# Hybrid attention block on one core: ring slots of 4352 bytes, a running sum of squares, and reordered score products

## The chip, the core and the metric

The kernel runs on one core of a Trainium2 chip. The core has a matrix engine (TensorE, PE in the rows; its weight loads are PEld), a vector engine (VectorE, DVE), an activation engine (ScalarE, ACT), GpSimd (POOL) and SyncE (SP), which here only issues the large loads. The engines run side by side, each through its own list of instructions, and wait for each other by semaphores. The metric is the time of one execution on the device in microseconds (us), lower is better.

## The reference, cut to what matters

```python
D_MODEL, SEQ, DEPTH = 2048, 256, 1            # one layer, one sequence of 256 tokens, fp32
h = rmsnorm(x, g_norm)                        # needs the sum of the squares of x, per token
z = einsum('bsd,dn->bsn', h, w_in)            # 2048 -> 12296 columns
# 8 heads of differential attention: q and k are two maps of 64 dims, v has 128
s = einsum('bqhmd,bkhmd->bhmqk', q, k) * scale ; p = softmax(causal(s))
a = p[:, :, 0] - lam * p[:, :, 1] ; oa = rmsnorm(a @ v, g_subln) * (1 - lam_init) * silu(ga)
# 8 heads of forgetting attention: q, k, v have 128 dims, a bias of cumulative log-forget gates
ob = softmax(causal(q @ k.T * scale + c_q - c_k)) @ v * silu(gb)
m = sigmoid(ma) * (oa @ w_proj_a) + sigmoid(mb) * (ob @ w_proj_b)
return rmsnorm(x + m @ w_out, g_final)
```

Queries are taken in two blocks of 128. The first block sees 128 keys, the second 256, so a map of scores is one block of 128x128 and one of 128x256.

## The kernel before, in words

**Precision.** Nearly all products are made three times with a rounded type (fp32r): both operands are split into a high part and a low part, and high x high, high x low and low x high are added in PSUM. That is `split_product` (lines 216 to 219): three matmuls, L217, L218 and L219. A few small products (transposes, values, sums) are plain fp32, for which the trace shows two weight loads and two matmul records each.

**The weight ring.** Weights come as tiles, numbered t = 0 to 255. A tile is 4096 bytes in each of 128 partitions (two blocks of 128 rows x 512 columns), and feeds 12 matmuls of 512 columns: 2 blocks, 2 halves of the tokens, 3 products. Tiles 8 to 11 hold 4 x 264 columns (4224 bytes), tiles 12 to 15 hold 4 x 256, each with 24 matmuls. Three buffers, `w_raw`, `w_hi` and `w_lo`, have four slots each, and tile t uses slot t % 4. SP loads tile t once VectorE has finished tile t-4 (`load`, line 186), ScalarE rounds it to `w_hi` once TensorE has finished tile t-4 (`split`, L421), VectorE subtracts to `w_lo` (`split`, L610), then TensorE uses both. A slot is `SLOT` elements long, the length of the longest tile: 1056, or 4224 bytes. In the built program `w_raw` begins 128 bytes past a multiple of 256, and so do `w_hi`, `w_lo`, `hT_hi` and `hT_lo` (the stationary operands) and `oT_hi` and `oT_lo`. 4224 is an odd multiple of 128. So slots 0 and 2 begin 128 past a multiple of 256, and slots 1 and 3 at a multiple of 256. Tiles 248 to 251, the first half of the last column block, are copied from the ring into `oT_hi` and `oT_lo` (L569, L817) and read there; their length in that buffer is 4096 bytes, so all four begin 128 past a multiple of 256.

**The first column block** (tiles 0 to 7, matmuls at L340) runs while x arrives. For each pair of row blocks ScalarE makes `hT_hi` (`x_part`, L433) and the tile's `w_hi`, VectorE makes `hT_lo` (L623) and `w_lo`. After that ScalarE squares all of x into `x_sq`, 8 pieces of 512 columns (L445; `x_sq` lies in the buffer `gates`), among the splits of tiles 8 to 11. VectorE adds the 16 blocks with one reduction (L641) to `x_ssq`. TensorE, between tiles 8 and 9, multiplies `x_ssq` by ones to sum over the partitions (L351). From this come `ms` (VectorE, L644) and `rstd` (GpSimd, L866), which every eviction of the first block needs.

**The column blocks c = 2 to 23** (8 tiles each) are the heads' projections and the merge gates. `attention(c, j)` puts the work of older heads between the tiles: after tile j = 1 the transposes, after tile j = 5 the products with the values of head c-3 (`values`, L285, 6 records) and the scores of head c-2 (`scores`, line 255). Heads 0 to 7 are the forgetting heads: one map, into PSUM bank B. Heads 8 to 15 are the differential heads: two maps, q and k in partitions 0 to 63 and 64 to 127, into banks B and C, the whole of B first. `head_qkT` (ScalarE, L474) and `head_qkT_lo` (VectorE, L693) make the high and low part of q and k of a head from bank A, 512 columns: q of both blocks, k of both blocks.

After that come 4 column blocks of the branch projections and 4 of the output projection, the last of them in another order (line 397).

Of the kernel before, what the change touches and what calls it, by code (L numbers as in the profile page):

```python
# [8 lines left out]
P = 128  # L9
D_MODEL = 2048  # L10
SEQ = 256
M_TILES = SEQ // P
KT = D_MODEL // P
HEADS = 8
HD = 128
QK = 64
# [5 lines left out]
CHUNK = 512  # L22
RING = 4
TILES = 8
Z_SLOTS = 3
FL_COLS = 2 * HD + HEADS
SLOT = 4 * FL_COLS
FL_COL = 8 * WIDTH
MERGE_COL = FL_COL + HEADS
N_HEADS = 2 * HEADS  # L30
# [11 lines left out]
def build(nc, x, xT, g_cols, consts_in, w_main, w_fl, g_final, out):  # L42
    fp32 = mybir.dt.float32
    fp32r = mybir.dt.float32r
    ALU = mybir.AluOpType
    ACT = mybir.ActivationFunctionType
    AX = mybir.AxisListType
# [6 lines left out]
    with ctx:  # L54
        def sb(name, shape, dt=fp32):
            return ctx.enter_context(nc.sbuf_tensor(name, shape, dt))
# [23 lines left out]
        lam_exp = sb("lam_exp", [P, 2])  # L80
        neg_half = sb("neg_half", [P, M_TILES])
        neg_lam = sb("neg_lam", [P, 1])
        x_ssq = sb("x_ssq", [P, SEQ])
        ms = sb("ms", [P, M_TILES])
        rstd = sb("rstd", [P, M_TILES])
        half_rstd = sb("half_rstd", [P, M_TILES])
# [2 lines left out]
        log_f = sb("log_f", [P, M_TILES, HEADS])  # L89
        c_nat = sb("c_nat", [P, M_TILES, HEADS])  # L90
        c_neg = sb("c_neg", [HEADS, SEQ])
        qkT_hi = sb("qkT_hi", [P, 4 * P], fp32r)
        qkT_lo = sb("qkT_lo", [P, 4 * P], fp32r)
        bias = sb("bias", [P, 3 * P])
        rope_t = sb("rope_t", [P, 4, M_TILES, 4, ROPE_HALF])
        probs = sb("probs", [P, 2, 3 * P])
# [21 lines left out]
        ones = consts[:, C_ONE:C_ONE + P]  # L118
# [6 lines left out]
        xT_sb = x_sb[:].rearrange("p (k n) -> p k n", k=KT)  # L125
        x_res = x_sb[:].rearrange("p (m n) -> p m n", m=M_TILES)
        x_sq = gates[:, 0, :].rearrange("p (k n) -> p k n", k=KT)
# [10 lines left out]
        A, B, C, Dk = bank("A"), bank("B"), bank("C"), bank("Dk")  # L138
# [12 lines left out]
        xh_ready, xl_ready, x_squared, x_summed = sem("xh_ready"), sem("xl_ready"), sem("x_squared"), sem("x_summed")  # L151
# [9 lines left out]
        qkT_done, qkT_hi_ready, qkT_ready = sem("qkT_done"), sem("qkT_hi_ready"), sem("qkT_ready")  # L161
# [9 lines left out]
        out_ready, out_stored = [sem("out_ready0"), sem("out_ready1")], sem("out_stored")  # L171

        def width(t):
            return SLOT if 8 <= t < 12 else 2 * CHUNK

        def raw_count(t):
            return 16 * (t // RING + 1)
# [37 lines left out]
        def _(pe):  # L215
            def split_product(acc, a_hi, a_lo, b_hi, b_lo, first, last):
                pe.matmul(acc, a_hi, b_hi, start=first, stop=False)  # L217
                pe.matmul(acc, a_hi, b_lo, start=False, stop=False)  # L218
                return pe.matmul(acc, a_lo, b_hi, start=False, stop=last)  # L219
# [35 lines left out]
            def scores(h):  # L255

                pe.wait_ge(qkT_ready, h + 1)
                if h >= 2:
                    pe.wait_ge(oT_lo_ready, h - 1)
                maps = 1 if h < HEADS else 2  # L260
                for i in range(maps):
                    part = slice(0, P) if maps == 1 else slice(i * QK, (i + 1) * QK)
                    S = (B, C)[i]
                    split_product(S[:, 0:P], qkT_hi[part, 0:P], qkT_lo[part, 0:P],
                                  qkT_hi[part, 2 * P:3 * P], qkT_lo[part, 2 * P:3 * P], True, True)
                    mm = split_product(S[:, P:3 * P], qkT_hi[part, P:2 * P], qkT_lo[part, P:2 * P],
                                       qkT_hi[part, 2 * P:4 * P], qkT_lo[part, 2 * P:4 * P], True, True)
                mm.then_inc(scores_done, 1)

            def prob_transposes(h):  # L270
# [54 lines left out]
            for j in range(TILES):  # L325
                hi, lo = k_view(w_hi, j, 2, CHUNK), k_view(w_lo, j, 2, CHUNK)
                for part, (x_part, w_part) in enumerate(((hT_hi, hi), (hT_lo, hi), (hT_hi, lo))):
                    for kk in range(2):
# [10 lines left out]
                        for m in range(M_TILES):  # L339
                            mm = pe.matmul(Z[m][:], x_part[:, 2 * j + kk, m * P:(m + 1) * P], w_part[:, kk],  # L340
                                           start=(j == 0 and part == 0 and kk == 0),
                                           stop=(j == TILES - 1 and part == 2 and kk == 1))
                mm.then_inc(w_used, 1)
            for j in range(4):
                tile(8 + j, 1, hT_hi, hT_lo, 4 * j, 4, FL_COLS, j == 0, j == 3)
                if j == 0:

                    pe.wait_ge(x_summed, 1)
                    pe.wait_ge(consts_loaded, 16)
                    for m in range(M_TILES):  # L350
                        mm = pe.matmul(A[:, m:m + 1], x_ssq[:, m * P:(m + 1) * P], ones[:, 0:1], start=True, stop=True)  # L351
                    mm.then_inc(ms_done, 1)
            banks_free(2)
            for j in range(4):
# [1 line left out]
            for c in range(2, PROJ):  # L356
                banks_free(fill_of(c))
                for j in range(TILES):
# [7 lines left out]
                    if c == 2 and j == 1:  # L366
                        pe.wait_ge(c_nat_ready, 1)
                        for m in range(M_TILES):
                            mm = pe.matmul(C[0:HEADS, m * P:(m + 1) * P], c_nat[:, m, :], ident, start=True, stop=True)
# [27 lines left out]
            for part, (m, y_cols, acc) in enumerate(LAST):  # L397
                tok = slice(m * P, (m + 1) * P)
                n = y_cols.stop - y_cols.start
                cols = slice(y_cols.start - 3 * CHUNK, y_cols.stop - 3 * CHUNK)  # L400
                for j in range(TILES):
                    t = 8 * (OUT + 3) + j
# [4 lines left out]
                    for kk in range(2):  # L407
                        k = 2 * j + kk
                        mm = split_product(acc[:, 0:n], hT_hi[:, k, tok], hT_lo[:, k, tok], hi[:, kk, cols],
                                           lo[:, kk, cols], k == 0, k == KT - 1)  # L410
# [3 lines left out]
        def _(act):  # L414
            def split(t):

                if t >= RING:
                    act.wait_ge(w_used, t - RING + 1)
                act.wait_ge(raw_loaded[t % RING], raw_count(t))
                n = width(t)  # L420
                act.activation(w_hi[:, t % RING, 0:n], w_raw[:, t % RING, 0:n], ACT.Copy).then_inc(hi_ready, 1)  # L421
# [6 lines left out]
            def x_part(j):  # L428

                act.wait_ge(x_loaded[j], 16)  # L430
                for kk in range(2):
                    k = 2 * j + kk
                    act.activation(hT_hi[:, k, :], xT_sb[:, k, :], ACT.Copy, scale=g_col[:, k:k + 1]).then_inc(xh_ready, 1)  # L433

            act.dma_start(g_col[:], g_cols).then_inc(g_loaded, 16)
            act.wait_ge(warm_ready, 1)
            act.activation(table_probe[:], warm[:, 0:1], ACT.Copy)
# [3 lines left out]
            for j in range(1, TILES):  # L441
                x_part(j)
                split(j)
            for j in range(TILES):
                act.activation(x_sq[:, 2 * j:2 * j + 2, :], xT_sb[:, 2 * j:2 * j + 2, :], ACT.Square,  # L445
                               scale=D_MODEL ** -0.5).then_inc(x_squared, 1)
                if j < 4:
                    split(8 + j)

            act.wait_ge(rstd_ready, 1)  # L450
            evacuate(0)
# [19 lines left out]
            def head_qkT(h):  # L471

                act.wait_ge(qkT_done, h + 1)
                act.activation(qkT_hi[:], A[:], ACT.Copy).then_inc(qkT_hi_ready, 1)  # L474

            def head_pT(h):
                act.wait_ge(pT_done, h + 1)
# [83 lines left out]
            for n in range(3):  # L561
                for j in range(TILES):
                    if n == 0 and j == 2:
                        merged_hi(3)
                    t = 8 * (OUT + n) + j + RING
# [26 lines left out]
        def _(dve):  # L592
# [13 lines left out]
            def split(t):  # L606

                dve.wait_ge(hi_ready, t + 1)
                n = width(t)
                dve.tensor_tensor(w_lo[:, t % RING, 0:n], w_raw[:, t % RING, 0:n], w_hi[:, t % RING, 0:n].bitcast(fp32),  # L610
                                  ALU.subtract).then_inc(lo_ready, 1)
# [6 lines left out]
            def x_part(j):  # L618

                for kk in range(2):  # L620
# [2 lines left out]
                    dve.scalar_tensor_tensor(hT_lo[:, k, :], xT_sb[:, k, :], g_col[:, k:k + 1], hT_hi[:, k, :].bitcast(fp32),  # L623
                                             ALU.mult, ALU.subtract).then_inc(xl_ready, 1)

            dve.memset(warm[:], 0.0).then_inc(warm_ready, 1)
            dve.memset(o_scale[:, 0:1], 0.5)
            dve.wait_ge(g_loaded, 16)
            for j in range(TILES):
# [5 lines left out]
                    dve.tensor_copy(w_hi[:, 0, CHUNK:2 * CHUNK], w_raw[:, 0, CHUNK:2 * CHUNK]).then_inc(hi_ready, 1)  # L635
                x_part(j)
                split(j)
            for j in range(3):
                split(8 + j)
            dve.wait_ge(x_squared, 8)  # L640
            dve.tensor_reduce(x_ssq[:], x_sq.rearrange("p k n -> p n k"), AX.X, ALU.add).then_inc(x_summed, 1)  # L641
            split(11)
            dve.wait_ge(ms_done, 1)
            dve.tensor_scalar(ms[:], A[:, 0:M_TILES], EPS, None, ALU.add).then_inc(ms_ready, 1)  # L644
            dve.wait_ge(rstd_ready, 1)
# [44 lines left out]

            def head_qkT_lo(h):
                dve.wait_ge(qkT_hi_ready, h + 1)
                dve.tensor_tensor(qkT_lo[:], A[:], qkT_hi[:].bitcast(fp32), ALU.subtract).then_inc(qkT_ready, 1)  # L693

            def gate_product(h):

# [286 lines left out]
```

## Time and profile before

| | us |
|---|---|
| median of 3 runs | 785.65 |
| lowest, highest | 785.4, 786.19 |
| the profiled execution, its own time | 785.83 |
| its span, first to last instruction | 784.0 |

| engine | busy us | share of the span |
|---|---|---|
| TensorE matmul | 766.0 | 98% |
| TensorE weight load | 633.1 | 81% |
| VectorE | 428.8 | 55% |
| ScalarE | 364.5 | 46% |
| GpSimd | 67.8 | 9% |

The profile gives busy time and the chain of work that ended last, of which TensorE has 95%. The mean clock granted to TensorE is 0.99 of full speed. Matmul records overlap (a record of 0.39 us begins 0.23 us after the one before), so what a matmul costs is read from start to start in the order of time, never from its duration.

### The profile page before, as it was taken

How to read it: one execution, taken by the hardware profiler on the slowest of the kernel's cores; microseconds unless marked ns; L12 is line 12 of the kernel's file. 1: busy time of each engine (PE TensorE's matmuls, PEld its weight loads, DVE VectorE, ACT ScalarE, POOL GpSimd, SP SyncE). 2: the span in 40 equal slices, each digit the busy share in tenths (PEclk: the TensorE clock that was granted, in tenths of full speed). 3: DMA queues.
4: the chain of work that ended last, by engine and by line, in shares of the span. 5: the costliest groups of instructions: out<-in, count | busy, mean ns of one | idle time of the engine just before them, and what ended most of it. 6: DMA issues, size and time to landing. Idle time of an engine off the chain costs nothing.

```text
span 784.0 us, 9598 instructions
## 1 busy us (share of the span) xinstructions
PE 766.0 (98%) x3652; PEld 633.1 (81%) x3652; DVE 428.8 (55%) x610; ACT 364.5 (46%) x540; POOL 67.8 (9%) x153
## 2 busy tenths in 40 slices
PE   8699999999999999999999999999999999999996
PEld 5598888888888888888888888888888888888886
DVE  6645555555555565666656564444444665655562
ACT  6535444444444454455455554434444434444441
POOL 0000200000001110222022000000000000001110
PEclk9989999999999999999999999999999999999998
DMA  8626655555555545645445545555555555865542
GB/s 320 217 82 218 238 169 179 168 174 171 170 178 169 175 164 165 183 159 168 162 161 183 163 164 187 187 190 188 188 188 188 191 186 187 308 210 186 189 154 108
DMA packets 39885, 143.80 MB, mean 183 GB/s; under 512 B 4568, under 2 KB 4576, under 8 KB 39328
## 3 DMA queue, kind: packets, MB, share of 16 engines
q1 hardware_dynamic: 39152, 140.85, 53.7%
q0 software_dynamic: 256, 1.54, 0.5%
q10 hardware_dynamic: 432, 0.79, 0.3%
q8 instruction: 30, 0.49, 0.3%
q14 instruction: 15, 0.12, 0.0%
HBM read 141.06 MB, written 2.11 MB: 183 GB/s over the span
## 4 chain that ended last, share of the span: by engine, by line
PE 95%; issue 2%; DVE 1%; DMA 1%; ACT 1%; SPq 0%; DVEq 0%; POOLq 0%; POOL 0%; ACTq 0%
PE Z L217 29%; PE Z L219 29%; PE Z L218 29%; PE Z L340 3%; PE A L285 1%; PE A L251 1%; DVE x_ssq L641 1%; DMA w_raw<-in_w_main 1%; PE Dk L276 1%; PE B L217 1%; PE B L218 0%; PE C L294 0%; PE B L219 0%; ACT gates L445 0%; ACT w_hi L421 0%
## 5 line engine op out<-in xcount | busy, mean ns | idle before, releaser
L610 DVE TENSOR_TENSOR w_lo<-w_raw,w_hi 128x1024 fp32r<-128x1024 f32 (+1 forms) x252 | 311.4, 1237 | 315.0 <-ACT w_hi L421 313.2
L421 ACT ACTIVATE w_hi<-w_raw 128x1024 fp32r<-128x1024 f32 (+1 forms) x247 | 261.9, 1061 | 364.9 <-PE Z L219 354.8
L217 PE MATMUL Z<-w_hi,hT_hi 128*128 128x512 f32 (+2 forms) x880 | 341.5, 388 | 0.5 <-DVE w_lo L610 0.5
L219 PE MATMUL Z<-w_hi,hT_lo 128*128 128x512 f32 (+2 forms) x880 | 338.7, 385 | 0.0
L218 PE MATMUL Z<-w_lo,hT_hi 128*128 128x512 f32 (+2 forms) x880 | 338.1, 384 | 0.0
L219 PEld LDWEIGHTS Z<-w_hi,hT_lo 128*128 128x128 f32 x880 | 166.2, 189 | 34.8
L217 PEld LDWEIGHTS Z<-w_hi,hT_hi 128*128 128x128 f32 x880 | 166.5, 189 | 34.3 <-issue 0.6
L218 PEld LDWEIGHTS Z<-w_lo,hT_hi 128*128 128x128 f32 x880 | 166.4, 189 | 33.4
L217 PE MATMUL Z<-w_hi,oT_hi 128*128 128x512 f32 x128 | 50.5, 394 | 0.0
L219 PE MATMUL Z<-w_hi,oT_lo 128*128 128x512 f32 x128 | 50.3, 393 | 0.0
L218 PE MATMUL Z<-w_lo,oT_hi 128*128 128x512 f32 x128 | 50.2, 392 | 0.0
L900 POOL TENSOR_TENSOR rope_t<-z_sb,consts 128x32 f32<-128x32 f32 x64 | 26.9, 453 | 88.1 <-DVE z_sb L615 48.4
L923 POOL TENSOR_TENSOR gates<-gates,rows 128x512 f32<-128x512 f32 x6 | 7.7, 1302 | 267.8 <-DVE gates L808 267.8
L219 PEld LDWEIGHTS Z<-w_hi,oT_lo 128*128 128x128 f32 x128 | 24.0, 188 | 5.5
L218 PEld LDWEIGHTS Z<-w_lo,oT_hi 128*128 128x128 f32 x128 | 24.0, 188 | 5.4
L217 PEld LDWEIGHTS Z<-w_hi,oT_hi 128*128 128x128 f32 x128 | 24.1, 188 | 5.3
L881 POOL TENSOR_TENSOR bias<-rows,c_nat 128x128 f32<-128x128 f32 (+1 forms) x16 | 7.7, 504 | 139.7 <-DVE neg_max L686 134.4
L916 POOL TENSOR_TENSOR o_rstd<-o_ms,neg_half 128x2 f32<-128x2 f32 x8 | 5.6, 702 | 119.2 <-DVE o_ms L764 119.2
L553 ACT ACTIVATE z_sb<-gates 128x512 f32<-128x512 f32 (+1 forms) x9 | 5.2, 579 | 22.7 <-DVE gates L834 13.9
L285 PEld LDWEIGHTS A<-z_sb,pT 128*128 128x128 f32 x96 | 13.1, 190 | 1.5
L425 ACT ACTIVATE z_sb<-Z,rstd 128x512 f32<-128x512 f32 x15 | 10.0, 668 | 9.2 <-POOL rstd L866 9.2
L285 PE MATMUL A<-z_sb,pT 128*128 128x128 f32 x96 | 13.3, 274 | 0.0
(155 smaller groups left out, 493.5 us busy)
## 6 DMA issues: line engine op xcount, KB each, us to landing
w_raw<-in_w_main SPq DMA_DIRECT2D x251, 512.0 KB, 3.3
w_raw<-in_w_fl SPq DMA_DIRECT2D x4, 528.0 KB, 5.2
x_sb<-in_xT SPq DMA_DIRECT2D x8, 256.0 KB, 6.4
x_sb<-in_x SPq DMA_DIRECT2D x1, 2048.0 KB, 11.2
rows<-c_rows_dram POOLq DMA_DIRECT2D x1, 1024.0 KB, 5.8
rows<-in_g_final SPq DMA_DIRECT2D x1, 1024.0 KB, 12.6
out_y<-gates SPq DMA_DIRECT2D x2, 384.0 KB, 2.5
out_y<-gates ACTq DMA_DIRECT2D x2, 384.0 KB, 3.5
```

What stands on the lines that cost most here:

```text
L217: pe.matmul(acc, a_hi, b_hi, start=first, stop=False)
L218: pe.matmul(acc, a_hi, b_lo, start=False, stop=False)
L219: return pe.matmul(acc, a_lo, b_hi, start=False, stop=last)
L251: mm = pe.transpose(A[:, (2 * i + m) * P:(2 * i + m + 1) * P], z_sb[:, h % Z_SLOTS, m, i * HD:(i + 1) * HD], ident)
L276: mm = pe.transpose(Dk[:, b * P:(b + 1) * P], probs[:, 0, b * P:(b + 1) * P], ident)
L285: mm = pe.matmul(A[:, q * P:(q + 1) * P], pT[:, b * P:(b + 1) * P], z_sb[:, h % Z_SLOTS, k, 2 * HD:3 * HD], start=b < 2, stop=b != 1)
L340: mm = pe.matmul(Z[m][:], x_part[:, 2 * j + kk, m * P:(m + 1) * P], w_part[:, kk], start=(j == 0 and part == 0 and kk == 0), stop=(j == TI ...
L421: act.activation(w_hi[:, t % RING, 0:n], w_raw[:, t % RING, 0:n], ACT.Copy).then_inc(hi_ready, 1)
L425: act.activation(z_sb[:, c % Z_SLOTS, 0], Z[2 * (fill_of(c) % 2)][:], ACT.Copy, scale=rstd[:, 0:1]).then_inc(evac[0], 1)
L610: dve.tensor_tensor(w_lo[:, t % RING, 0:n], w_raw[:, t % RING, 0:n], w_hi[:, t % RING, 0:n].bitcast(fp32), ALU.subtract).then_inc(lo_ready, 1)
L641: dve.tensor_reduce(x_ssq[:], x_sq.rearrange("p k n -> p n k"), AX.X, ALU.add).then_inc(x_summed, 1)
L900: ins = pool.tensor_tensor(rope_t[:, i, m], u, v, ALU.mult)
```

## The change

`SLOT` goes from 1056 to 1088 elements, from 4224 to 4352 bytes, 17 x 256; the tiles' lengths stay. All slots now begin 128 bytes past a multiple of 256. `x_ssq` has two blocks of 256 columns. ScalarE squares two row blocks at a time inside the first column block (`x_square`), VectorE adds each piece to `x_ssq` (`x_sum`, 7 adds of 512 columns) in place of the reduction, and TensorE's product with ones follows tile 9 in place of tile 8, with two matmuls for each half of the tokens in place of one. In `scores`, the block of 128x128 is one plain fp32 matmul of `qk0T`, a new copy of q and k of the first block, in place of three fp32r matmuls; the 128x256 block keeps its three, and for differential heads the matmuls of B and C alternate. `head_qkT` writes `qk0T` (256 columns) and a `qkT_hi` of 384 columns, `head_qkT_lo` a `qkT_lo` of 384.

```diff
-SLOT = 4 * FL_COLS
+SLOT = 1088
...
-                maps = 1 if h < HEADS else 2
-                for i in range(maps):
-                    part = slice(0, P) if maps == 1 else slice(i * QK, (i + 1) * QK)
-                    S = (B, C)[i]
-                    split_product(S[:, 0:P], qkT_hi[part, 0:P], qkT_lo[part, 0:P],
-                                  qkT_hi[part, 2 * P:3 * P], qkT_lo[part, 2 * P:3 * P], True, True)
-                    mm = split_product(S[:, P:3 * P], qkT_hi[part, P:2 * P], qkT_lo[part, P:2 * P],
-                                       qkT_hi[part, 2 * P:4 * P], qkT_lo[part, 2 * P:4 * P], True, True)
+                parts = [slice(0, P)] if h < HEADS else [slice(0, QK), slice(QK, 2 * QK)]
+                for S, part in zip((B, C), parts):
+                    pe.matmul(S[:, 0:P], qk0T[part, 0, :], qk0T[part, 1, :], start=True, stop=True)
+                for n, (q, k) in enumerate(((qkT_hi, qkT_hi), (qkT_hi, qkT_lo), (qkT_lo, qkT_hi))):
+                    for S, part in zip((B, C), parts):
+                        mm = pe.matmul(S[:, P:3 * P], q[part, 0:P], k[part, P:3 * P], start=n == 0, stop=n == 2)
...
-                if j == 0:
-
-                    pe.wait_ge(x_summed, 1)
+                if j == 1:
+
+                    pe.wait_ge(x_summed, TILES - 1)
                     pe.wait_ge(consts_loaded, 16)
                     for m in range(M_TILES):
-                        mm = pe.matmul(A[:, m:m + 1], x_ssq[:, m * P:(m + 1) * P], ones[:, 0:1], start=True, stop=True)
+                        for i in range(2):
+                            mm = pe.matmul(A[:, m:m + 1], x_ssq[:, i, m * P:(m + 1) * P], ones[:, 0:1], start=i == 0, stop=i == 1)
...
-                act.activation(qkT_hi[:], A[:], ACT.Copy).then_inc(qkT_hi_ready, 1)
+                act.activation(qk0T[:], A[:].rearrange("p (i n) -> p i n", i=2)[:, :, 0:P], ACT.Copy)
+                act.activation(qkT_hi[:], A[:, P:4 * P], ACT.Copy).then_inc(qkT_hi_ready, 1)
...
+            def x_sum(j):
+
+                dve.wait_ge(x_squared, j + 1)
+                if j > 1:
+                    dve.wait_ge(x_summed, j - 1)
+                before = x_sq[:, 0:2, :] if j == 1 else x_ssq[:]
+                dve.tensor_tensor(x_ssq[:], before, x_sq[:, 2 * j:2 * j + 2, :], ALU.add).then_inc(x_summed, 1)
...
-            for j in range(3):
+                if j > 3:
+                    x_sum(j - 3)
+            for j in range(4):
                 split(8 + j)
-            dve.wait_ge(x_squared, 8)
-            dve.tensor_reduce(x_ssq[:], x_sq.rearrange("p k n -> p n k"), AX.X, ALU.add).then_inc(x_summed, 1)
-            split(11)
+                if j < 3:
+                    x_sum(j + 5)
```

On VectorE, from the last split of the first column block on, the program stood like this (128x1056 are the splits of tiles 8 to 11):

```order
20 L610 TENSOR_TENSOR w_lo<-w_raw,w_hi 128x1024
21 L610 TENSOR_TENSOR w_lo<-w_raw,w_hi 128x1056 x3
22 L641 TENSOR_REDUCE x_ssq<-gates 128x256
23 L610 TENSOR_TENSOR w_lo<-w_raw,w_hi 128x1056
24 L644 TENSOR_SCALAR ms<-A 128x2
```

and now, from the fifth tile (t = 4) on:

```order
14 L617 TENSOR_TENSOR w_lo<-w_raw,w_hi 128x1024
15 L639 TENSOR_TENSOR x_ssq<-gates 128x512
16 L630 SCALAR_TENSOR_TENSOR hT_lo<-x_sb,g_col,hT_hi 128x256 x2
17 L617 TENSOR_TENSOR w_lo<-w_raw,w_hi 128x1024
18 L639 TENSOR_TENSOR x_ssq<-x_ssq,gates 128x512
...
29 L617 TENSOR_TENSOR w_lo<-w_raw,w_hi 128x1056
30 L639 TENSOR_TENSOR x_ssq<-x_ssq,gates 128x512
31 L617 TENSOR_TENSOR w_lo<-w_raw,w_hi 128x1056
32 L660 TENSOR_SCALAR ms<-A 128x2
```

The one reduction ahead of the split of tile 11 has become seven adds, one behind each split of tiles 4 to 10.

On TensorE, the scores of a differential head, before:

```order
1142 L285 MATMUL A<-z_sb,pT 128x128 x3
1143 L217 MATMUL B<-qkT_hi 128x128
1144 L218 MATMUL B<-qkT_lo,qkT_hi 128x128
1145 L219 MATMUL B<-qkT_hi,qkT_lo 128x128
1146 L217 MATMUL B<-qkT_hi 128x256
1147 L218 MATMUL B<-qkT_lo,qkT_hi 128x256
1148 L219 MATMUL B<-qkT_hi,qkT_lo 128x256
1149 L217 MATMUL C<-qkT_hi 128x128
1150 L218 MATMUL C<-qkT_lo,qkT_hi 128x128
1151 L219 MATMUL C<-qkT_hi,qkT_lo 128x128
1152 L217 MATMUL C<-qkT_hi 128x256
1153 L218 MATMUL C<-qkT_lo,qkT_hi 128x256
1154 L219 MATMUL C<-qkT_hi,qkT_lo 128x256
```

and now:

```order
1126 L284 MATMUL A<-z_sb,pT 128x128 x3
1127 L263 MATMUL B<-qk0T 128x128
1128 L263 MATMUL C<-qk0T 128x128
1129 L266 MATMUL B<-qkT_hi 128x256
1130 L266 MATMUL C<-qkT_hi 128x256
1131 L266 MATMUL B<-qkT_lo,qkT_hi 128x256
1132 L266 MATMUL C<-qkT_lo,qkT_hi 128x256
1133 L266 MATMUL B<-qkT_hi,qkT_lo 128x256
1134 L266 MATMUL C<-qkT_hi,qkT_lo 128x256
1135 L218 MATMUL Z<-w_hi,hT_hi 128x512
```

Twelve matmuls of one bank after the other have become two plain fp32 matmuls (two records each in a trace) and six fp32r matmuls that alternate between the banks.

## Rows read from the trace of the kernel before

**Rows 1.** Page, part 1: busy time, share of the span, instructions of each engine.

```profile
PE 766.0 (98%) x3652; PEld 633.1 (81%) x3652; DVE 428.8 (55%) x610; ACT 364.5 (46%) x540; POOL 67.8 (9%) x153
```

**Rows 2.** Waits of TensorE, longest first: total us, times, longest us.

```profile
PE A L351 <- DVE x_ssq L641: 7.4, 1, 7.4
```

**Rows 3.** Order of time, 20 to 42 us: start, duration, engine, line, idle before.

```profile
20.08 1.21 DVE L610 TENSOR_TENSOR w_lo<-w_raw,w_hi 128x1024 fp32r<-128x1024 f32 x1
...
22.01 1.21 DVE L610 TENSOR_TENSOR w_lo<-w_raw,w_hi 128x1024 fp32r<-128x1024 f32 x1
...
31.14 2.17 ACT L445 ACTIVATE gates<-x_sb 128x512 f32<-128x512 f32 x4
...
33.35 7.00 DVE L641 TENSOR_REDUCE x_ssq<-gates 128x256 f32<-128x4096 f32 x1 [3.61 <-ACT gates L445]
...
40.41 1.02 PE L351 MATMUL A<-consts,x_ssq 128*128 128x1 f32 x4 [7.39 <-DVE x_ssq L641]
41.29 0.57 PE L217 MATMUL Z<-w_hi,hT_hi 128*128 128x264 f32 x1
```

**Rows 4.** Order of time, TensorE: first matmuls of tiles 10, 11 and 12.

```profile
46.46 0.28 PE L217 MATMUL Z<-w_hi,hT_hi 128*128 128x264 f32 x1
...
49.40 0.28 PE L217 MATMUL Z<-w_hi,hT_hi 128*128 128x264 f32 x1
...
52.35 0.28 PE L217 MATMUL Z<-w_hi,hT_hi 128*128 128x256 f32 x1
```

**Rows 5.** Stretches: us, busy of PE, PEld, DVE, ACT, POOL, PEclk, DMA share, GB/s.

```profile
41.00:44.00 3.00, 3.00 (x14) 3.00 (x15) 1.44 (x4) 1.47 (x2) 0.72 (x1) 0.50 0.48 152
48.00:52.00 4.00, 4.00 (x35) 4.00 (x34) 0.00 (x0) 0.00 (x0) 0.00 (x0) 1.00 0.02 5
```

**Rows 6.** Order of time, TensorE: first matmuls of tiles 240, 241 and 242.

```profile
732.07 0.39 PE L217 MATMUL Z<-w_hi,hT_hi 128*128 128x512 f32 x1
...
734.80 0.40 PE L217 MATMUL Z<-w_hi,hT_hi 128*128 128x512 f32 x1
...
737.60 0.39 PE L217 MATMUL Z<-w_hi,hT_hi 128*128 128x512 f32 x1
```

**Rows 7.** Same view, the last column block: starts of tiles 249, 250, 253, 254.

```profile
755.55 0.39 PE L217 MATMUL Z<-oT_hi,hT_hi 128*128 128x512 f32 x1
...
756.91 0.39 PE L217 MATMUL Z<-oT_hi,hT_hi 128*128 128x512 f32 x1
...
760.99 0.40 PE L217 MATMUL Z<-w_hi,hT_hi 128*128 128x512 f32 x1
...
762.38 0.39 PE L217 MATMUL Z<-w_hi,hT_hi 128*128 128x512 f32 x1
```

**Rows 8.** Same view, values and scores of forgetting heads.

```profile
130.98 0.83 PE L285 MATMUL A<-z_sb,pT 128*128 128x128 f32 x6
131.56 0.31 PE L217 MATMUL B<-qkT_hi 128*128 128x128 f32 x1
...
132.34 0.40 PE L217 MATMUL Z<-w_hi,hT_hi 128*128 128x512 f32 x1
```

**Rows 9.** Same view, values and scores of differential heads.

```profile
403.80 0.83 PE L285 MATMUL A<-z_sb,pT 128*128 128x128 f32 x6
404.56 0.32 PE L217 MATMUL B<-qkT_hi 64*128 64x128 f32 x1
...
404.84 0.32 PE L217 MATMUL C<-qkT_hi 64*128 64x128 f32 x1
404.94 0.33 PE L217 MATMUL B<-qkT_hi 64*128 64x256 f32 x1
...
405.52 0.28 PE L219 MATMUL C<-qkT_hi,qkT_lo 64*128 64x256 f32 x1
405.72 0.50 PE L217 MATMUL Z<-w_hi,hT_hi 128*128 128x512 f32 x1
```

**Rows 10.** Groups by line and shape: busy us, mean ns of one, idle before.

```profile
L693 DVE TENSOR_TENSOR qkT_lo<-A,qkT_hi 128x512 fp32r<-128x512 f32 x16 | 10.8, 676 | 0.0
...
L478 ACT ACTIVATE pT<-Dk 128x384 f32<-128x384 f32 x16 | 7.7, 482 | 0.0
```

More of the change, by code:

```diff
@@ L82, in build @@
         neg_lam = sb("neg_lam", [P, 1])
-        x_ssq = sb("x_ssq", [P, SEQ])
+        x_ssq = sb("x_ssq", [P, 2, SEQ])
         ms = sb("ms", [P, M_TILES])
@@ L91, in build @@
         c_neg = sb("c_neg", [HEADS, SEQ])
-        qkT_hi = sb("qkT_hi", [P, 4 * P], fp32r)
-        qkT_lo = sb("qkT_lo", [P, 4 * P], fp32r)
+        qk0T = sb("qk0T", [P, 2, P])
+        qkT_hi = sb("qkT_hi", [P, 3 * P], fp32r)
+        qkT_lo = sb("qkT_lo", [P, 3 * P], fp32r)
         bias = sb("bias", [P, 3 * P])
@@ L173, in width @@
         def width(t):
-            return SLOT if 8 <= t < 12 else 2 * CHUNK
+            return 4 * FL_COLS if 8 <= t < 12 else 2 * CHUNK
         def raw_count(t):
@@ L433, in x_part, with x_square @@
                     act.activation(hT_hi[:, k, :], xT_sb[:, k, :], ACT.Copy, scale=g_col[:, k:k + 1]).then_inc(xh_ready, 1)
+            def x_square(j):
+                act.activation(x_sq[:, 2 * j:2 * j + 2, :], xT_sb[:, 2 * j:2 * j + 2, :], ACT.Square,
+                               scale=D_MODEL ** -0.5).then_inc(x_squared, 1)
             act.dma_start(g_col[:], g_cols).then_inc(g_loaded, 16)
@@ L443, in _ @@
                 split(j)
[L444 to L448, printed above, removed]
+                if j > 1:
+                    x_square(j - 2)
+            for j in range(4):
+                if j < 2:
+                    x_square(j + TILES - 2)
+                split(8 + j)
             act.wait_ge(rstd_ready, 1)
@@ L624, in x_part @@
                                              ALU.mult, ALU.subtract).then_inc(xl_ready, 1)
+            def x_sum(j):
+                dve.wait_ge(x_squared, j + 1)
+                if j > 1:
+                    dve.wait_ge(x_summed, j - 1)
+                before = x_sq[:, 0:2, :] if j == 1 else x_ssq[:]
+                dve.tensor_tensor(x_ssq[:], before, x_sq[:, 2 * j:2 * j + 2, :], ALU.add).then_inc(x_summed, 1)
             dve.memset(warm[:], 0.0).then_inc(warm_ready, 1)
@@ L637, in _ @@
                 split(j)
-            for j in range(3):
+                if j > 3:
+                    x_sum(j - 3)
+            for j in range(4):
                 split(8 + j)
-            dve.wait_ge(x_squared, 8)
-            dve.tensor_reduce(x_ssq[:], x_sq.rearrange("p k n -> p n k"), AX.X, ALU.add).then_inc(x_summed, 1)
-            split(11)
+                if j < 3:
+                    x_sum(j + 5)
             dve.wait_ge(ms_done, 1)
@@ L692, in head_qkT_lo @@
                 dve.wait_ge(qkT_hi_ready, h + 1)
-                dve.tensor_tensor(qkT_lo[:], A[:], qkT_hi[:].bitcast(fp32), ALU.subtract).then_inc(qkT_ready, 1)
+                dve.tensor_tensor(qkT_lo[:], A[:, P:4 * P], qkT_hi[:].bitcast(fp32), ALU.subtract).then_inc(qkT_ready, 1)
             def gate_product(h):
```

## The prediction

> **What bounds the kernel now.** First the page: TensorE is busy for 766.0 of 784.0 us, the next engine for 55% of them [rows 1]. So a change pays where it shortens TensorE's own row of work, or an idle stretch in it. The waits come next: TensorE has one long one, 7.4 us, for the sum of squares [rows 2]. The order of time tells why. ScalarE ends its last squares at 33.3, VectorE's reduction starts at 33.35 and takes 7.00, and TensorE begins the product with ones at 40.41 [rows 3]. Then I look at what TensorE is granted: behind that idle stretch the clock is 0.50, which is 1.2 GHz, and from 48 us on it is 1.00, which is 2.4 GHz [rows 5]. The same 24 matmuls that take 2.94 and 2.95 us in tiles 10 and 11 (46.46 to 49.40 to 52.35) take 5.17 in tile 9 (41.29 to 46.46) [rows 3, 4]. Last come the steady tiles, from first matmul to first matmul. Tile 240 (slot 0) takes 2.73 us, tile 241 (slot 1) 2.80 with the same 12 matmuls [rows 6]; unrounded, the starts of the 20 tiles from 228 on give 2.735 and 2.792 in turn, with no wait between. This is the largest thing that the busy shares hide.
>
> **1. Slots of 4352 bytes.** Is it the slot's address that costs the odd tiles 0.057 us, or their place in the operands, which alternates in the same way? The last column block answers. Tile 249 is odd, but is read from another buffer, 128 bytes past a multiple of 256 like slots 0 and 2; six of its matmuls take 1.36 us (755.55 to 756.91). Tile 253, also odd, is read from slot 1, and six take 1.39 (760.99 to 762.38) [rows 7]. The address it is, and the two fast kinds (slots 0 and 2) lie 256 apart modulo 512, so that a multiple of 256 between slots is enough. The bases of the three ring buffers and of the stationary operands keep their place modulo 256. All four slots then are of the fast kind. Odd tiles of 512 columns in the ring: 124 from t = 1 to 247, less 9, 11, 13 and 15 with narrower matmuls (even and odd alike there [rows 4]) = 120. 120 x 0.057 = 6.8, and 0.06 in tiles 253 and 255: **-6.9 us**. All of it is on the path, since the rows of TensorE have no gaps there. Bounds: 0, if it isn't the address after all, and -6.9. I take -6.9, by [rows 7].
> By the Trainium skill ("TensorE: Matmul & The Clock Gate", section "Back-to-back issue gap") a matmul of N columns follows the one before by N/2.4 + 2.5 ns at full clock, 216 ns at 512, with no word on addresses. Here it is 228 in one kind of slot and 233 in the other, so no run here agrees with it; by that rule the slots would bring nothing.
>
> **2. The sum of squares.** Removed: the stretch without work, 7.5 us (tile 8 would be over at about 32.9, the product starts at 40.41), and the slow tile 9, 5.17 - 2.94 = 2.2 us. Added on TensorE: the product with ones is 4 records, 0.88 us from 40.41 to 41.29 at the low clock [rows 3], and is now 8 records. At full clock a plain fp32 record of 128 weights takes 0.112 (six in L285 and six in the scores fill 1.36 us [rows 8]), so 8 x 0.112 = 0.9, as much as before; the other bound is 8 x 0.22 = 1.8, if the low clock came back.
> Is something late in place of the reduction? *ScalarE* has one piece of squares more in each step, 2.17 / 4 = 0.54 [rows 3]. Its step and VectorE's are both 1.93 us (20.08 to 22.01), so its becomes 2.47. *VectorE* gets an add of 512 columns. The trace has none from SBUF alone; the nearest row is a subtraction of 512 with one operand in PSUM, 0.68 [rows 10], the upper bound the one of 1024, 1.21 [rows 3]. I take 0.6 from start to start: 2.53. TensorE needs 2.74 a tile, so both still keep ahead. In full: VectorE ended tile 7's split at 23.2 and will at about 25.9 (ScalarE's five squares more are 2.7 us); TensorE wants that tile's low part at 28.9. ScalarE waits for TensorE to release the slots of tiles 10 and 11 anyway, so these splits stay at about 28.5 to 29.9 and 30 to 31. The seventh add ends at about 32.3, and TensorE is through tile 9 at 35.6: 3.3 us to spare. With adds at 1.2 each the sum would be 4.2 us later, 0.9 too late. The loads of tiles 8 to 11, queued on SP behind VectorE's splits, go out 1.1 to 2.7 us later; what uses them has 3 us. Behind tile 9 `ms`, `rstd` and the two evictions take some 2.5 us and run under tiles 10 and 11 (5.9 us), with room for the split of tile 12. From tile 12 on the order is the old one, shifted. TensorE gets there at 42.4 in place of 52.35; 0.2 of that belongs to part 1. **-9.7 us**, bounds -10 and -8.
>
> **3. The fp32 block, forgetting heads.** From the first record of the values to the tile behind the scores it is 1.36 us [rows 8] for 12 records, 0.113 each, 128 or 256 columns alike. One fp32 matmul is two records, three fp32r are three: one record less, 8 x -0.113 = **-0.9 us**. Two copies on ScalarE (256 columns at about 0.46, 384 at 0.48 [rows 10]) take the place of one, 0.3 us more for each head, but the scores come four tiles later, and VectorE's subtraction gets shorter. Cost nothing.
>
> **4. Differential heads.** The values start at 403.80 and the next tile at 405.72: 1.92 us for 6 + 12 records [rows 9]. C's first matmul starts at 404.84, ahead of B's fourth (404.94), though it stands behind it in the program. So two halves of the array do run side by side, but C lags B by 0.28. Now each bank has 5 records. Around them stands what I keep [rows 9]: values' last record at 404.35; 0.20 to 0.25 to the first score; 0.20 from the last score's start (405.52) to the tile. If C follows B by one record (0.112), it is 0.25 + 4 x 0.112 + 0.112 + 0.20 = 1.02 in place of 1.37 (404.35 to 405.72): -0.35 for a head. With no lag -0.46 to -0.51, with the old lag of 0.28 -0.18, with no overlap at all (10 records in a row, 1.47) +0.1. I take one record, since B's two fp32 records stand ahead of C's in the program: 8 x -0.35 = **-2.8 us**, bounds -4.1 and +0.8.
> The Trainium skill says (same page, "Part 3: Packing small matmuls", "The mechanism") that matmuls start strictly in program order, and those on different row groups some 4 ns apart. The order of time contradicts the first half [rows 9]. By the second the pairs would start together, and this part would be at its bound, 1.3 us below my sum.
>
> **Sum.** -6.9 - 9.7 - 0.9 - 2.8 = -20.3. The profiled execution took 785.83 in all, 784.0 of it span; 785.83 - 20.3 = 765.5. The median of the runs lies 0.2 lower: **765.4 us**.
>
> **Rivals.**
> *A. The alternating scores don't overlap.* In its favour: entering the half-array products and leaving them costs 0.1 us more than a record each time [rows 9], and alternation could pay something like it often. Against: B and C overlap already. Part 4 is +0.8: 769.0. Chance 0.13.
> *B. The slots bring nothing*, because it is another relation between ring and stationary operand that counts. For: four slots become four addresses modulo 1024, of which the trace shows two. Against: the pair of odd tiles [rows 7]. 765.4 + 6.9 = 772.3. Chance 0.07. With it goes the case that the change doesn't do what it says and makes all slots slow, 779: 0.02.
> *C. Slower than before: TensorE starves in the first column block and loses its clock.* If VectorE's add took over 0.81 us, its step would exceed 2.74 and every tile from 4 on would wait. A wait alone is cheap, under 2 us in all. But at 1.2 GHz, half the clock, a tile of 512 columns takes up to twice its 2.74 us: six tiles at +2.5 and four narrow ones at +2.2 (part 2) are 24 us, and 765.4 + 24 = 789. It decides at that 0.81, and only if short waits lower the clock. Against: 0.68 is the dearer kind [rows 10], and only a wait of 7.4 us has brought the low clock. Chance 0.02.
>
> **Numbers.** My forecast has the chance 0.76, from 763.6 (no lag, and a little more) to 768 (old lag, late adds, dear product). With A the range of 763.6 to 770.0 leaves out B, C and a tail, some 15%. A measurement of this kernel can tell about 0.2% from no change, 1.6 us; every case but C is below that. Faster 0.97, same 0.01, slower 0.02.
>
> **What would show it.** In the changed kernel's order of time: tiles of odd number at 2.735 us like even ones (part 1; 2.79 or other values in some slots would be B). No wait of TensorE for `x_ssq`, a clock of 1.00 from 33 to 52 us and tile 12 at about 42.4 (part 2; a wait between tiles 4 and 9 would be the start of C). 1.24 us from the values to the tile for a forgetting head (part 3), about 1.57 for a differential one, with C's first record about 0.11 behind B's (part 4; 2.0 would be A). I would be wrong if a wait that the 7.4 us has covered so far came up, such as that for the constants' load, or if the ring's loads, closer together now, landed late.

## The result and the profile after

| | before | after |
|---|---|---|
| median of 4 runs each, us | 785.66 | 762.18 |
| lowest, highest | 785.4, 786.19 | 761.63, 764.31 |
| profiled execution: own time, span | 785.83, 784.0 | 761.63, 759.8 |

The ratio is 0.9705, with a 95% interval of 0.9686 to 0.9725: 23.5 us less. The forecast was 765.4 with a range of 763.6 to 770.0. The sign and the four sources were right, but the time lies 1.4 us below the range, so the forecast was wrong in size. Of the runs reported below, one of the slots alone (1549 us) and one of the kernel before beside it (4355 us) fell far out of line, and medians, ratios and intervals are of the others.

The page of the changed kernel begins like this (busy time of each engine, then the longest wait of TensorE; its line numbers differ by a few from those before, L218 to L220 are the three products):

```profile
PE 749.2 (99%) x3632; PEld 627.0 (83%) x3632; DVE 422.8 (56%) x616; ACT 365.9 (48%) x556; POOL 76.2 (10%) x153
```

```profile
PE Dk L322 <- DVE warm L641: 1.3, 1, 1.3
```

The wait of 7.4 us [rows 2] is gone and none has taken its place: the longest is 1.3 us, at the very start, and behind the first column block there is one of 0.44 us, ahead of tile 13. In the order of time, the product with ones and the first matmuls of tiles 10, 11 and 12 (start, duration):

```profile
34.83 0.95 PE L351 MATMUL A<-consts,x_ssq 128*128 128x1 f32 x8
35.63 0.37 PE L218 MATMUL Z<-w_hi,hT_hi 128*128 128x264 f32 x1
...
38.66 0.28 PE L218 MATMUL Z<-w_hi,hT_hi 128*128 128x264 f32 x1
...
41.56 0.29 PE L218 MATMUL Z<-w_hi,hT_hi 128*128 128x256 f32 x1
```

Tile 12 starts at 41.56, where it started at 52.35 [rows 4]. In the view of stretches (us, busy of PE, PEld, DVE, ACT, POOL, granted clock, DMA share, GB/s) the clock of this part is full, 2.4 GHz, where it was 0.50 [rows 5]:

```profile
33.00:36.00 3.00, 3.00 (x28) 3.00 (x27) 0.16 (x1) 0.00 (x0) 0.00 (x0) 1.00 0.70 251
41.00:44.00 3.00, 3.00 (x27) 3.00 (x27) 1.08 (x4) 1.74 (x4) 0.00 (x0) 1.00 0.44 160
```

The first matmuls of tiles 240, 241 and 242, which answer to [rows 6]:

```profile
708.26 0.39 PE L218 MATMUL Z<-w_hi,hT_hi 128*128 128x512 f32 x1
...
710.98 0.39 PE L218 MATMUL Z<-w_hi,hT_hi 128*128 128x512 f32 x1
...
713.70 0.39 PE L218 MATMUL Z<-w_hi,hT_hi 128*128 128x512 f32 x1
```

Both tiles take 2.72 us. The odd one has lost 0.07, and the even one 0.015, which I had not forecast. With the stage boundaries of both traces the difference can be laid out, in us:

| from, to | before | after | difference | in my sum |
|---|---|---|---|---|
| start, tile 1 | 10.50 | 9.87 | -0.63 | 0 |
| tile 1, tile 12 | 41.85 | 31.69 | -10.16 | -9.9 |
| tile 12, tile 248 | 701.82 | 688.47 | -13.36 | -10.3 |
| tile 248, end of the span | 29.84 | 29.80 | -0.04 | -0.1 |

The difference of the two spans is 24.2 us, 0.7 more than that of the medians. Of the 3.9 us by which my sum of 20.3 falls short of 24.2, 3.1 are in the steady tiles, 0.6 ahead of tile 1 and 0.3 between tiles 1 and 12.

### The profile page after: what moved, and what is told of

The parts are those of the page before. It is cut to its first block, busy times and chain, and to the rows that moved or that the text cites. A ratio compares the mean times of both kernels' runs of the same rounds, so it can differ in the third digit from the quotient of the medians.

```text
span 759.8 us, 9586 instructions
## 1 busy us (share of the span) xinstructions
PE 749.2 (99%) x3632; PEld 627.0 (83%) x3632; DVE 422.8 (56%) x616; ACT 365.9 (48%) x556; POOL 76.2 (10%) x153
## 4 chain that ended last, share of the span: by engine, by line
PE 96%; issue 2%; DMA 1%; DVE 0%; ACT 0%; SPq 0%; DVEq 0%; POOLq 0%; POOL 0%; ACTq 0%
PE Z L218 29%; PE Z L220 29%; PE Z L219 29%; PE Z L339 3%; PE A L284 1%; PE A L252 1%; DMA w_raw<-in_w_main 1%; PE B L266 1%; PE Dk L275 1%; PE B L263 1%; PE C L293 0%; ACT w_hi L421 0%; PE A L301 0%; PE B L301 0%; DVE w_lo L617 0%
## 5 line engine op out<-in xcount | busy, mean ns | idle before, releaser
L218 PE MATMUL Z<-w_hi,hT_hi 128*128 128x512 f32 (+2 forms) x880 | 337.8, 384 | 0.4 <-DVE w_lo L617 0.4
L220 PE MATMUL Z<-w_hi,hT_lo 128*128 128x512 f32 (+2 forms) x880 | 335.3, 381 | 0.0
L218 PEld LDWEIGHTS Z<-w_hi,hT_hi 128*128 128x128 f32 x880 | 165.4, 188 | 32.1 <-issue 0.6
L220 PEld LDWEIGHTS Z<-w_hi,hT_lo 128*128 128x128 f32 x880 | 165.4, 188 | 31.8
L218 PE MATMUL Z<-w_hi,oT_hi 128*128 128x512 f32 x128 | 50.1, 391 | 0.0
L220 PE MATMUL Z<-w_hi,oT_lo 128*128 128x512 f32 x128 | 49.9, 389 | 0.0
L220 PEld LDWEIGHTS Z<-w_hi,oT_lo 128*128 128x128 f32 x128 | 24.0, 188 | 5.0
L218 PEld LDWEIGHTS Z<-w_hi,oT_hi 128*128 128x128 f32 x128 | 24.0, 188 | 4.8
L902 POOL TENSOR_TENSOR bias<-bias,consts 128x128 f32<-128x128 f32 x16 | 15.2, 971 | 0.6
```

The lines of the kernel that those rows point to most:

```text
L902: pool.tensor_tensor(bias[:, sl], bias[:, sl], mask, ALU.add).then_inc(bias_ready, 1)
```

## Experiments: each part alone

Each of these is the kernel before with one of the edits.

**Slots of 4352 bytes alone.**

```diff
-SLOT = 4 * FL_COLS
+SLOT = 1088
...
-            return SLOT if 8 <= t < 12 else 2 * CHUNK
+            return 4 * FL_COLS if 8 <= t < 12 else 2 * CHUNK
```

> The kernel before with slots of 4352 bytes and nothing else. Theory S (my price was too small: a tile read from slots 1 or 3 also slows the first matmuls of the tile behind it): even tiles go from 2.735 to 2.720 us as odd ones go from 2.792 to 2.720, and 120 pairs are worth 120 x 0.087 = 10.4 us: 775.2. Theory P (the price on record, 6.9 us, and the rest came from the start of the execution or from the mix of the edits): 778.8, with even tiles at 2.735.

Measured: 775.72, ratio 0.9877 (0.9859 to 0.9894), 10.0 us less than the 785.73 beside it. Tiles 240, 241 and 242 in its order of time:

```profile
722.31 0.39 PE L217 MATMUL Z<-w_hi,hT_hi 128*128 128x512 f32 x1
...
725.03 0.39 PE L217 MATMUL Z<-w_hi,hT_hi 128*128 128x512 f32 x1
...
727.75 0.39 PE L217 MATMUL Z<-w_hi,hT_hi 128*128 128x512 f32 x1
```

Even and odd tiles are at 2.72. The interval in us is 8.3 to 11.1, which excludes the 6.9 of my sum and holds the 10.4 of theory S. From tile 1 to tile 248 the rows give -10.1; 0.2 of it is a shorter tile 9, which both kernels run at the low clock (4.94 us here, 5.17 before), and need not come from the slots. So a slow tile had also slowed the tile behind it.

**The squares alone.** The edit is the one shown in the change: `x_square`, `x_sum`, and the product with ones behind tile 9.

> The kernel before with the squares added tile by tile alone. My sum had 9.7 us for it: 775.9, with no wait of TensorE for the sum, a clock of 1.00 behind it, and 8 records of 0.11 us for the product with ones. Rival: the stage gave more than that, 10.5 us or more (775.2 or less), because TensorE also gets into the first tiles sooner.

Measured: 776.37, ratio 0.9883 (0.9868 to 0.9899), -9.4 us. Tile 12 starts 32.05 us behind tile 1, where it was 41.85: -9.8. My 9.7 was right. The rival's larger gain is not there: tile 1 began later here (10.82) than in the kernel before.

**The fp32 block alone**, one map after the other:

```diff
-                maps = 1 if h < HEADS else 2
...
+                parts = [slice(0, P)] if h < HEADS else [slice(0, QK), slice(QK, 2 * QK)]
+                for S, part in zip((B, C), parts):
+                    pe.matmul(S[:, 0:P], qk0T[part, 0, :], qk0T[part, 1, :], start=True, stop=True)
+                    for n, (q, k) in enumerate(((qkT_hi, qkT_hi), (qkT_hi, qkT_lo), (qkT_lo, qkT_hi))):
+                        mm = pe.matmul(S[:, P:3 * P], q[part, 0:P], k[part, P:3 * P], start=n == 0, stop=n == 2)
```

> The kernel before with the first score block in fp32, the differential maps one bank after the other. By a price of 0.113 us for each record less: 8 x 0.113 for the forgetting heads and 16 x 0.113 less what overlaps for the differential ones, -1.8 to -2.7 us: 783.0 to 783.9. Rival: a change between fp32 and fp32r costs time in itself, some 0.05 us at each, and the gain is under 1.2 us: 784.5 or more.

Measured: 783.03, ratio 0.9964 (0.9951 to 0.9977), -2.7 us. From the start of the tile ahead of values and scores to the second tile start behind them (two tiles, since the scores also change the first steps of the tile behind them) it is 6.787 in place of 6.887 us for a forgetting head (-0.100) and 7.433 in place of 7.580 for a differential one (-0.147): 8 x 0.247 = 2.0 us by the rows, which the interval (1.8 to 3.9) holds. The rival falls. The rows are the better measure, since something else varied as well: tile 9 behind the stall takes 4.38 us in this trace, 4.54 in that of the next run and 5.17 before, though no edit touches it.

**In turn alone**, all products still in fp32r:

```diff
+                parts = [slice(0, P)] if h < HEADS else [slice(0, QK), slice(QK, 2 * QK)]
+                for q0, k1 in ((0, 3), (1, 4)):
+                    for n, (q, k) in enumerate(((qkT_hi, qkT_hi), (qkT_hi, qkT_lo), (qkT_lo, qkT_hi))):
+                        for S, part in zip((B, C), parts):
+                            mm = pe.matmul(S[:, P * q0:P * (2 * q0 + 1)], q[part, q0 * P:(q0 + 1) * P],
+                                           k[part, 2 * P:k1 * P], start=n == 0, stop=n == 2)
```

> The kernel before with the differential maps in turn, all six products of a map kept in fp32r. If the alternating matmuls of B and C start in pairs, the lag of 0.28 us is gone: 8 x -0.28 = -2.2 us, 783.4. If they run one after the other it is the same time as before or slower: 785.6 or more.

Measured: 782.72, ratio 0.9965 (0.9950 to 0.9979). The same two tiles take 7.300 us for a differential head, -0.280, the old lag of 0.28 to the hundredth; for the forgetting heads they are unchanged at 6.887. The changed kernel shows how, values and scores in its order of time:

```profile
385.92 0.83 PE L284 MATMUL A<-z_sb,pT 128*128 128x128 f32 x6
386.68 0.37 PE L263 MATMUL B<-qk0T 64*128 64x128 f32 x1
386.69 0.37 PE L263 MATMUL C<-qk0T 64*128 64x128 f32 x1
386.89 0.27 PE L263 MATMUL B<-qk0T 64*128 64x128 f32 x1
386.90 0.27 PE L263 MATMUL C<-qk0T 64*128 64x128 f32 x1
...
387.24 0.27 PE L266 MATMUL B<-qkT_hi,qkT_lo 64*128 64x256 f32 x1
387.25 0.27 PE L266 MATMUL C<-qkT_hi,qkT_lo 64*128 64x256 f32 x1
387.45 0.50 PE L218 MATMUL Z<-w_hi,hT_hi 128*128 128x512 f32 x1
```

B and C start 0.01 us apart at each step. I had expected a lag of one record. On the other hand the two fp32 records of a bank stand 0.21 apart and not 0.112. Taking them in turn isn't the reason: with the fp32 block alone, one bank after the other, they are 0.21 apart too (0.112 for a forgetting head, on the whole array). The stretch from the values to the tile is 1.53 us, where it was 1.92 [rows 9].

## Experiments: what the address does

Each of these is the changed kernel with unused bytes between buffers, or another slot length.

**Everything moved by 128 bytes.**

```diff
+        pad = sb("pad", [P, 32])
         w_raw = sb("w_raw", [P, RING, SLOT])
```

> The changed kernel with 128 unused bytes ahead of the ring, so that slots and stationary operands all begin at a multiple of 256. Theory R (what counts is where the slot lies against the stationary operand; both are shifted together): tiles stay at 2.720 us, 762. Theory Q (what counts is the slot's own address, a multiple of 256 is slow): every tile of 512 columns costs 2.79 us or more, 240 x 0.07 = 17 us more, 779.

Measured: 762.16, tiles at 2.720. The changed kernel once more, in the same group of runs, gave 762.45.

**Only the stationary operands moved** (and the buffers behind them), the same line ahead of `hT_hi`.

> The changed kernel with 128 unused bytes between the ring and the stationary operands: slots 128 bytes past a multiple of 256 as in the changed kernel, stationary operands at a multiple of 256. Theory R: every tile is slow, 2.79 us or more, about 779. Theory Q: nothing changes, 762.

Measured: 777.13, ratio 0.9893 (0.9876 to 0.9909), 14.7 us above the changed kernel; the tiles take 2.780 to 2.800 us. The starts of tiles 162, 163 and 164 in its order of time:

```profile
502.34 0.39 PE L219 MATMUL Z<-w_hi,hT_hi 128*128 128x512 f32 x1
...
505.13 0.40 PE L219 MATMUL Z<-w_hi,hT_hi 128*128 128x512 f32 x1
...
507.91 0.40 PE L219 MATMUL Z<-w_hi,hT_hi 128*128 128x512 f32 x1
```

These two runs decide it. A slot at a multiple of 256 is slow beside operands that begin 128 past one [rows 6], and fast beside operands that begin at one. A slot 128 past one is fast in the changed kernel and slow here. The trace of this slow kernel has a control: tiles 248 to 251 are read from `oT_hi` and `oT_lo`, which moved along with `hT_hi` and `hT_lo`, and there six matmuls take 1.36 us, while those of tiles 252 to 255, from the ring, take 1.39 to 1.40. What counts is the distance between the streamed and the stationary operand modulo 256 bytes. Theory Q, which is how the prediction had put it, falls, though it gives the same for this change.

**Slots of 4288 bytes** (`SLOT = 1072`).

> The changed kernel with slots of 4288 bytes: slots 0, 1, 2, 3 begin 128, 64, 0 and 192 bytes past a multiple of 256. Both theories: slot 0 fast (less the 0.015 us that a slow tile leaves to the next), slot 2 slow. What is asked is slots 1 and 3, 64 bytes off either way: slow too (then only the multiple of 256 helps: about 762 + 180 x 0.06 = 773), or between.

Measured: 773.74, near the 773 expected for one good slot of four, but not slot by slot. Tiles 205 to 208 (slots 1, 2, 3, 0) take 2.800, 2.790, 2.751 and 2.745 us in its trace, so a slot 64 bytes behind the operands is as slow as one 128 off, and one 64 bytes ahead is cheaper, but not free. Even the good slot is at 2.745; it follows a slow one.

**The changed kernel once more.**

> The changed kernel once more, on the chip of the three others, as what they are compared with: 762.2, tiles at 2.720. The start of tile 1 on TensorE came at 9.87 us here and at 10.50 in the kernel before; if that belongs to the change it comes at 9.87 again, if it is scatter of the first loads it comes anywhere from 9.8 to 11.2.

Measured: 762.45, ratio 0.9705 (0.9691 to 0.9719). Tile 1 starts at 10.72 us. In the thirteen other traces of this study, it starts anywhere from 9.63 to 11.22, with the arrival of the first loads, in kernels whose first instructions are the same. The 0.63 us of the first stage are scatter and no part of the change.

**Which operand?** `w_lo` alone 128 bytes off, and then `hT_lo` alone, each with a gap ahead of it and one behind it.

```diff
+        pad = sb("pad", [P, 32])
         w_lo = sb("w_lo", [P, RING, SLOT], fp32r)
+        pad2 = sb("pad2", [P, 32])
         hT_hi = sb("hT_hi", [P, KT, SEQ], fp32r)
```

> The changed kernel with w_lo alone 128 bytes off (two gaps of 128 unused bytes, ahead of w_lo and behind it; every other tensor as before modulo 256). w_lo is the streamed operand of the second of three products (L219). Theory own (a matmul is slow when its own two operands differ modulo 256): only the step from L219 to L220 grows, by 6 to 7 ns, a tile is 2.74 to 2.75 us, the time 762.3 + 240 x 0.027 = 769. Theory next (slow when the weights of the next matmul, loaded meanwhile, differ from the operand now streaming): the same step, the same time; the next run tells the two apart. Rival: any one misaligned buffer slows all three products: 779.

> The changed kernel with hT_lo alone 128 bytes off. hT_lo is the stationary operand of the third product (L220), loaded while the second (L219) streams. Theory own: the step behind L220 grows. Theory next: the step behind L219 grows, L220's own does not. Either way about 2.745 us for the tiles that use hT_lo (all of 512 columns but the 32 of the branch projections, which stay at 2.720), and 762.3 + 208 x 0.027 = 768.

Measured: 776.62 with `w_lo` off, 772.30 with `hT_lo` off. Both of my prices were too low. With `w_lo` off, in the order of time (here L220 to L222 are the three products, L221 streams `w_lo`):

```profile
500.19 0.40 PE L221 MATMUL Z<-w_lo,hT_hi 128*128 128x512 f32 x1
500.43 0.39 PE L222 MATMUL Z<-w_hi,hT_lo 128*128 128x512 f32 x1
500.66 0.40 PE L220 MATMUL Z<-w_hi,hT_hi 128*128 128x512 f32 x1
500.89 0.40 PE L221 MATMUL Z<-w_lo,hT_hi 128*128 128x512 f32 x1
```

Unrounded, the steps behind L221, L222 and L220 are 0.234, 0.230 and 0.236 us, where 0.227 is the fast one. So all three products are slow, with one of the four buffers off, which is the rival's form, though at less than its 779. This holds for about half of the undisturbed tiles, at 2.800 us; the others take 2.773, those of the output projection nearly all, with steps of 0.227 to 0.235, and the runs don't say why. With `hT_lo` off the steps behind the products are 0.234 (the one that uses it), 0.233 (the one during which it is loaded) and 0.227: both theories name one of the two, neither names both, and the rival falls here. A tile is 2.773, and in the branch projections, which don't read `hT_lo`, 2.720. That is as far as it goes: a matmul is slowed by its own operands and by those of its neighbours, which fits a slow tile that reaches into the next one. That reach was three steps in the kernel before, and neither it nor the mechanism in the memory or in TensorE is settled by these runs.

## Experiments: the stall and its clock

**The product with ones later, the reduction as it was** (the kernel before, otherwise unchanged):

```diff
-                if j == 0:
+                if j == 1:
```

> The kernel before with TensorE's product with ones behind tile 9 in place of tile 8, and the reduction as it was. The reduction ends at 40.4 all the same, TensorE is through tile 9 at 35.8, so the wait is 4.7 us and not 7.4. Theory A: the clock stays high over a wait of that length, and the gain is 2.9 + 2.2 = 5.1 us: 780.6. Theory B: the clock falls as it did, the slow stretch moves to tile 10, and the gain is 2.9 only: 782.8.

Measured: 782.57, ratio 0.9968 (0.9956 to 0.9981), -2.8 us. Its longest wait of TensorE, and a stretch behind it (columns as above):

```profile
PE A L351 <- DVE x_ssq L641: 4.6, 1, 4.6
```

```profile
41.00:44.00 3.00, 3.00 (x14) 3.00 (x15) 1.53 (x4) 1.38 (x2) 0.72 (x1) 0.50 0.44 127
```

The wait is shorter by 2.8 us, but the clock is at 0.50 again, and now tile 10 is the slow one, 4.27 us in place of 2.94. Theory B holds, and the 5.1 us of theory A lie outside the interval (1.5 to 3.5): 4.6 us without work still cost the clock. But the slow stretch has no fixed price. Here it ends within tile 10 (from 44.07 us on the matmuls follow each other by 0.12 and not 0.22 us) and costs 1.3 us; before it cost tile 9 2.2. So from tile 1 to tile 12 this trace is 3.8 us shorter, more than theory B's 2.9. Moving the wait hides a part of it; only the sum that is ready in time removes the slow tile too. The tile-by-tile adds did this with 3.9 us to spare (VectorE, the last two adds and the split between them; the last add is over at 30.92, and TensorE comes to the product with ones at 34.83):

```profile
28.47 0.68 DVE L639 TENSOR_TENSOR x_ssq<-x_ssq,gates 128x512 f32<-128x512 f32 x1
29.07 1.25 DVE L617 TENSOR_TENSOR w_lo<-w_raw,w_hi 128x1056 fp32r<-128x1056 f32 x1
30.24 0.68 DVE L639 TENSOR_TENSOR x_ssq<-x_ssq,gates 128x512 f32<-128x512 f32 x1
```

**Two more edits on the changed kernel.** VectorE folds the two blocks of `x_ssq`, which have been added apart, and the split of tile 13 goes ahead of the evictions of the narrow tiles on both engines.

```diff
+                if j == 2:
+                    dve.wait_ge(x_summed, TILES - 1)
+                    dve.tensor_tensor(x_ssq[:, 0, :], x_ssq[:, 0, :], x_ssq[:, 1, :], ALU.add).then_inc(x_summed, 1)
...
             split(12)
+            split(13)
             act.wait_ge(w_used, 12)
...
-            split(13)
             act.activation(fl_abs[:], fl[:], ACT.Abs).then_inc(act_step, 1)
```

> The changed kernel with two more edits: VectorE adds the two blocks of x_ssq (256 columns) so that the product with ones is 4 records and not 8, and the split of tile 13 stands ahead of the evictions of the narrow tiles on ScalarE and VectorE. Expected: the product 0.93 - 4 x 0.112 = 0.48 us, the wait of TensorE ahead of tile 13 (0.62 us) gone: tile 14 starts 1.1 us sooner, 761.3. Rival: the wait comes back ahead of tile 14, whose split then stands behind the chain of the forget gates: 761.9.

Measured: 762.19, ratio 0.9707 (0.9692 to 0.9721). The time can't tell it from the changed kernel (762.18 and 762.45): its interval is 2 us wide, and the start scatters by as much as the gain. The rows can: the product is four records, and the two waits of TensorE that the profile lists (1.3 and 1.2 us) both lie ahead of tile 2.

```profile
35.24 0.50 PE L350 MATMUL A<-consts,x_ssq 128*128 128x1 f32 x4
35.60 0.37 PE L218 MATMUL Z<-w_hi,hT_hi 128*128 128x264 f32 x1
```

From the start of tile 1 to that of tile 14 it is 37.04 us, in the changed kernel 38.11: 1.07 us less, as worked out. A faster kernel by its rows, then, but not shown by its time.

## Why the prediction was wrong in size, point by point

**The slots: right cause, wrong price, and this is the miss.** The term was -6.9. The stages give -9.9: the -13.36 of the steady tiles less 3.8 for the heads, and 0.4 in the other stages, some of it in tiles 10 and 11, 0.04 to 0.05 us each, which I had left out as narrow. The step that failed is "all four slots then are of the fast kind", priced at what an even tile took, 2.735 us. But an even tile stood behind a slow one: in an unrounded trace of before its first three steps are 0.231 to 0.233 us and the other nine 0.227. An undisturbed tile takes 12 x 0.2267 = 2.720. The row that said so was in front of me: tile 249 of [rows 7], which does not follow a ring slot directly, needs 1.36 us for six matmuls, 2.72 for twelve. I used it to show that the address counts, and didn't notice that it is faster than the tile that I took as the measure. 240 x 0.015 us are 3.6, of which some 0.6 did not come. A part was lost where scores stand between two tiles: with the new slots alone, such a pair of tiles gained 0.053 us for a forgetting head and 0.080 for a differential one, where an undisturbed pair gained 0.087. Rival B, that the slots bring nothing, is refuted; its reason, that the relation of the ring to the stationary operand counts, holds all the same.

**The squares: right**, -9.7 forecast, -9.8 in the rows. VectorE's add takes 0.60 from start to start (28.47 to 29.07), as I took it. The product with ones takes 0.80 to the next tile's start (34.83 to 35.63) and some 0.1 more in that tile's first step, the 0.9 forecast. A part of the agreement is luck: the 2.2 us for the slow tile were one execution's value, and the same code cost 1.4 and 1.6 us in the traces of the fp32 block and of the maps in turn. Rival C, a TensorE that starves in the first column block, is refuted: its condition was an add of over 0.81.

**The fp32 block: right.** -0.113 a head was forecast for forgetting heads; alone it is -0.100, and in the changed kernel -0.094 (the two tiles take 6.833 us with the new slots alone, and 6.740 with all). The stretch from the values to the tile is 0.112 shorter with the fp32 block alone, as forecast, and the tile behind gives 0.012 of it back.

**The differential heads: about right, by two errors.** -0.35 a head was forecast, -0.387 measured (7.500 with the new slots alone, 7.113 with all), 3.1 us in all. There is no lag between the banks, which my lower bound had, where I took 0.11; but the five records of a bank, steps of 0.21, 0.03, 0.20 and 0.12, take 0.56 from first to last and not 4 x 0.112 = 0.45. The first score stands 0.21 behind the last value record, where I took 0.25 (and my terms add up to 1.01, not 1.02). That these nearly cancel is luck. Done alone, the two edits gave -0.147 and -0.280 a head; done together, 0.04 less than this sum. Rival A (no overlap) is refuted.

**The range** took its lower end from a missing lag of the banks and gave the slots no room below: their lower bound was also the value that I took. I had called -6.9 both.

## What to carry to other kernels

Where the same matmuls take two different times in alternation, compare addresses of the streamed and the stationary buffer modulo 256 bytes, and lay out rings so that every slot begins at the same place as the stationary operand; here a 128-byte longer slot was worth 10 us of 785. As the price of the undisturbed case take a tile that has undisturbed neighbours, not the faster of two that alternate. A reduction that stands at the end of a stage is best added up inside it when the engine has slack in each step, since the wait costs the clock behind it too.

## What the runs showed of the hardware that I had not expected

- Matmuls of 512 fp32r columns follow each other by 0.2267 us when streamed and stationary operand begin at the same place modulo 256 bytes, and by 0.232 to 0.233 on average when they are 128 apart. Whether that place is 0 or 128 makes no difference (762.16 and 762.45 us). At 64 bytes to either side a tile took 2.75 and 2.80 us.
- One buffer off out of four slows its neighbours too: all three steps for `w_lo` in half of the tiles, two of three for `hT_lo`.
- Matmuls on the two halves of the array that are issued in turn start 0.01 us apart, with the second fp32 pair 0.21 us behind the first. In turn or not, the two fp32 records of a bank stand 0.21 apart on half of the array, and 0.112 on the whole.
- A wait of TensorE of 4.6 us was followed by the 1.2 GHz clock just as one of 7.4 us was. How long the low clock then lasted differed: it cost the tiles behind the wait 1.3 us in one trace and 2.2 in another.
